# The chunk inverse of a delta-rule recurrence: levels over half the columns, one half of the state kept in PSUM

## The reference

```python
def step(S, inp):
    r_t, w_t, k_t, v_t, kk_t, b_t = inp
    Sa = jnp.einsum('bhij,bhj->bhi', S, -kk_t)
    S = S * w_t[:, :, None, :] + Sa[..., None] * b_t[:, :, None, :] + v_t[..., None] * k_t[:, :, None, :]
    return S, jnp.einsum('bhij,bhj->bhi', S, r_t)

S_final, y = lax.scan(step, wkv0.astype(f32), seq_in)
```

## Time and profile before

| | |
|---|---|
| median of three executions | 1726.22 us |
| the profiled execution, its own time | 1722.33 us |
| its span | 1720.5 us |
| PE busy | 1581.8 us, 92% |
| DVE busy | 1009.6 us, 59% |
| ACT busy | 843.4 us, 49% |
| POOL busy | 578.6 us, 34% |
| mean granted PE clock | 0.974 of 2.4 GHz |

### The profile page before, as it was taken

The page is one execution under the profiler, slowest core; times in us unless marked ns, Lnnn a source line. Parts: engine busy times, 40 slices in busy tenths (PEclk is TensorE's granted clock), DMA queues, the critical chain, the costliest instruction groups (busy, mean ns, idle before and its releaser), DMA issues. The chain is left out here.

```text
span 1720.5 us, 41466 instructions
## 1 busy us (share of the span) xinstructions
PE 1581.8 (92%) x17389; PEld 1499.4 (87%) x17389; DVE 1009.6 (59%) x1718; ACT 843.4 (49%) x1480; POOL 578.6 (34%) x393
## 2 busy tenths in 40 slices
PE   4999999989799899999789999999897989899996
PEld 4999999987588789999789999989776878899995
DVE  3534368695798665443354434968677877544433
ACT  2545455756444555444344444656663446554431
POOL 0433412102266433444233433020215553344440
PEclk9999999999899999999989999999998999999998
DMA  5555557452144445555355555644603463456540
GB/s 174 161 173 177 177 151 220 129 173 79 48 121 124 138 155 176 169 195 178 112 158 173 178 176 183 194 134 145 184 1 101 128 182 101 148 172 196 178 166 26
DMA packets 280490, 256.28 MB, mean 149 GB/s; under 512 B 48022, under 2 KB 268540, under 8 KB 280290
## 3 DMA queue, kind: packets, MB, share of 16 engines
q1 hardware_dynamic: 276538, 252.05, 47.0%
q10 hardware_dynamic: 3768, 1.59, 0.4%
HBM read 242.22 MB, written 11.38 MB: 147 GB/s over the span
## 5 line engine op out<-in xcount | busy, mean ns | idle before, releaser
L223 PE MATMUL ps<-front_h_hi,front_hi 128*128 128x264 f32 x1520 | 447.4, 294 | 35.1 <-DVE front_lo L210 31.2
L224 PE MATMUL ps<-front_h_lo,front_hi 128*128 128x264 f32 x1520 | 436.9, 287 | 0.0
L225 PE MATMUL ps<-front_h_hi,front_lo 128*128 128x264 f32 x1520 | 436.5, 287 | 0.0
L210 POOL TENSOR_TENSOR front_lo<-front_raw,front_hi 128x1024 fp32r<-128x1024 f32 (+2 forms) x90 | 217.5, 2416 | 574.2 <-ACT front_hi L203 574.2
L203 ACT ACTIVATE front_hi<-front_raw 128x1024 fp32r<-128x1024 f32 (+2 forms) x238 | 246.7, 1039 | 274.7 <-PE ps L225 237.0
L223 PEld LDWEIGHTS ps<-front_h_hi,front_hi 128*128 128x128 f32 x1520 | 291.6, 192 | 44.8 <-issue 41.2
L210 POOL TENSOR_TENSOR out_lo<-out_raw,out_hi 128x1024 fp32r<-128x1024 f32 (+1 forms) x84 | 198.8, 2369 | 310.8 <-ACT out_hi L203 310.8
L224 PEld LDWEIGHTS ps<-front_h_lo,front_hi 128*128 128x128 f32 x1520 | 291.9, 192 | 0.8
L225 PEld LDWEIGHTS ps<-front_h_hi,front_lo 128*128 128x128 f32 x1520 | 290.2, 191 | 0.1
L203 ACT ACTIVATE out_hi<-out_raw 128x1024 fp32r<-128x1024 f32 (+1 forms) x168 | 173.2, 1038 | 220.9 <-PE ps L225 178.0
L210 DVE TENSOR_TENSOR front_lo<-front_raw,front_hi 128x1024 fp32r<-128x1024 f32 (+1 forms) x148 | 180.0, 1217 | 118.7 <-ACT front_hi L203 118.7
(11 more groups left out here) (375 smaller groups left out, 3346.9 us busy)
## 6 DMA issues: line engine op xcount, KB each, us to landing
front_raw<-in_w_in SPq DMA_DIRECT2D x50, 1024.0 KB, 5.3
front_raw<-in_ffn_w_in SPq DMA_DIRECT2D x44, 1024.0 KB, 5.7
out_raw<-in_ffn_w_in SPq DMA_DIRECT2D x44, 1024.0 KB, 5.6
back_sample_rows<-row_scratch SPq DMA_DIRECT2D x160, 128.0 KB, 3.0
out_raw<-in_w_out SPq DMA_DIRECT2D x16, 1024.0 KB, 6.3
front_raw<-in_ffn_w_out SPq DMA_DIRECT2D x16, 896.0 KB, 4.6
out_raw<-in_ffn_w_out SPq DMA_DIRECT2D x16, 896.0 KB, 4.6
front_raw<-in_ffn_w_out SPq DMA_DIRECT2D x8, 1024.0 KB, 5.0
```

The costliest lines, as they stand in the source:

```text
L210: eng.tensor_tensor(self.lo[n % self.RING][:, 0:k, 0:w], self._raw(n), self.hi[n % self.RING][:, 0:k, 0:w].bitcast(F32), ALU.subtract).the ...
L223: pe.matmul(out, hi[:, j, 0:w], x_hi[:, j], start=start and j == 0, stop=False)
L224: pe.matmul(out, hi[:, j, 0:w], x_lo[:, j], start=False, stop=False)
L225: mm = pe.matmul(out, lo[:, j, 0:w], x_hi[:, j], start=False, stop=stop and j == k - 1)
```

## The change

Five things change, all in `back_stage`, for both layers.

- Level `i` only fills the columns of the early half of every block pair in `x` and of the late half in `xt`. `part_of(a, i, late)` picks these 32 of every 64 columns, in runs of `b` columns. `level_t1` and both products of `level_u` now stream 32 columns in place of 64; their number stays.
- `t1` gets one buffer per level (`t1_pair`, `t1_rest`), set to zero once by POOL; `t1_copy` writes only the early half.
- `turn_x` writes bank UB and leaves its accumulation open. The U product adds to it there (`add=True`), so `x` is summed up in PSUM.
- DVE's addition to `x` goes. In its place `x_update(l, i)` on ACT copies the changed half of bank UB to `x`; it stands directly ahead of `t1_copy(l, i + 1)`. `level_t1(l, i + 1)` waits for it by `x_in`.
- DVE's addition to `xt` covers half the columns.

```diff
+    def part_of(a, i, late):
+        b = LEVELS[i]
+        return a.rearrange("p (n two t) -> p n two t", two=2, t=b)[:, :, late]
+
+    columns = lambda a: a.rearrange("p q t -> p (q t)")
...
-        t1 = st.sb("n_x", [P, 4, C])
+        t1_pair = st.sb("n_x_first", [P, 2, 4, C])
+        t1_rest = at("n_x_rest", 71296, [P, LV - 2, 4, C])
+        t1 = lambda i: t1_pair[:, i] if i < 2 else t1_rest[:, i - 2]
...
+                pool.memset(t1_pair[:], 0.0).then_inc(s("t1_zero"), 1)
                 for g in range(RT + 1):
                     l = g - 1
+                    if g == 1:
+                        pool.wait_ge(s("tok_ps"), 2)
+                        pool.memset(t1_rest[:], 0.0).then_inc(s("t1_zero"), 1)
...
-                    act.activation(t1[:].rearrange("p q t -> p (q t)"), ps[:, T1B, 0:4 * C], ACT.Copy).then_inc(s("t1_in"), 1)
+                    if p == 0:
+                        act.wait_ge(s("t1_zero"), 1 if i < 2 else 2)
+                    act.activation(part_of(columns(t1(i)), i, 0), part_of(ps[:, T1B, 0:4 * C], i, 0), ACT.Copy).then_inc(s("t1_in"), 1)
...
+                def x_update(p, i):
+                    act.wait_ge(s("u_ps"), (LV - 1) * p + i + 1)
+                    act.activation(part_of(columns(x[:, p % 2]), i, 0), part_of(ps[:, UB, 0:4 * C], i, 0), ACT.Copy).then_inc(s("x_in"), 1)
...
                     if 0 <= l < RT:
+                        x_update(l, 0)
                         t1_copy(l, 1)
...
                     if 0 <= l < RT:
+                        x_update(l, 3)
                         t1_copy(l, 4)
                         rv_copy(l)
...
                 def update(p, i):
-                    four = lambda b: ps[:, b, 0:4 * C].rearrange("p (q t) -> p q t", q=4)
-                    if i < LV - 1:
-                        ...
-                        dve.tensor_tensor(x[:, p % 2], x[:, p % 2], four(UB), ALU.add).then_inc(s("x_up"), 1)
                     dve.wait_ge(s("ut_ps"), LV * p + i + 1)
                     if i:
                         dve.wait_ge(s("xt_up"), LV * p + i)
-                    dve.tensor_tensor(xt[:, p % 3], xt[:, p % 3], four(UB + 1), ALU.add).then_inc(s("xt_up"), 1)
+                    changed = part_of(columns(xt[:, p % 3]), i, 1)
+                    dve.tensor_tensor(changed, changed, part_of(ps[:, UB + 1, 0:4 * C], i, 1), ALU.add).then_inc(s("xt_up"), 1)
...
-                def blocks(at, left, right):
+                def blocks(at, left, right, i, late, add=False):
+
                     for q in range(4):
                         for w in half:
-                            mm = pe.matmul(ps[w, at, q * C:(q + 1) * C], left[w, q], right[w, q], start=True, stop=True)
+                            mm = pe.matmul(part_of(ps[w, at, q * C:(q + 1) * C], i, late), left[w, q], part_of(right[w, q], i, late),
+                                           start=not add, stop=True, skip_group_check=add)
...
                     if p:
-                        pe.wait_ge(s("t1_in"), LV * p)
+                        pe.wait_ge(s("x_in"), LV * p)
...
                     pe.wait_ge(s("lev_done"), n + 1)
-                    if i:
-                        pe.wait_ge(s("x_up"), (LV - 1) * p + i)
+                    pe.wait_ge(s("x_in"), n + 1)
+                    if n:
                         pe.wait_ge(s("t1_in"), n)
-                    else:
-                        pe.wait_ge(s("x_in"), p + 1)
-                    blocks(T1B, lev[:, n % 2], x[:, p % 2]).then_inc(s("t1_ps"), 1)
+                    blocks(T1B, lev[:, n % 2], x[:, p % 2], i, 0).then_inc(s("t1_ps"), 1)
```

More of the change, by code:

```diff
@@ L1674, in t1_copy @@
                         act.wait_ge(s("ut_ps"), n)
-                    act.activation(t1[:].rearrange("p q t -> p (q t)"), ps[:, T1B, 0:4 * C], ACT.Copy).then_inc(s("t1_in"), 1)
+                    if p == 0:
+                        act.wait_ge(s("t1_zero"), 1 if i < 2 else 2)
+                    act.activation(part_of(columns(t1(i)), i, 0), part_of(ps[:, T1B, 0:4 * C], i, 0), ACT.Copy).then_inc(s("t1_in"), 1)
                 def x_copy(p):
                     act.wait_ge(s("x_ps"), p + 1)
-                    act.activation(x[:, p % 2].rearrange("p q t -> p (q t)"), ps[:, T1B, 0:4 * C], ACT.Copy).then_inc(s("x_in"), 1)
+                    act.activation(columns(x[:, p % 2]), ps[:, UB, 0:4 * C], ACT.Copy).then_inc(s("x_in"), 1)
+                def x_update(p, i):
+                    act.wait_ge(s("u_ps"), (LV - 1) * p + i + 1)
+                    act.activation(part_of(columns(x[:, p % 2]), i, 0), part_of(ps[:, UB, 0:4 * C], i, 0), ACT.Copy).then_inc(s("x_in"), 1)
                 def rv_copy(p):
@@ L1789, in _ @@
                     if 0 <= l < RT:
+                        x_update(l, 1)
                         t1_copy(l, 2)
@@ L1800, in _ @@
                     if 0 <= l < RT:
+                        x_update(l, 2)
                         t1_copy(l, 3)
@@ L1875, in update @@
                 def update(p, i):
-                    four = lambda b: ps[:, b, 0:4 * C].rearrange("p (q t) -> p q t", q=4)
-                    if i < LV - 1:
-                        dve.wait_ge(s("u_ps"), (LV - 1) * p + i + 1)
-                        if i:
-                            dve.wait_ge(s("x_up"), (LV - 1) * p + i)
-                        else:
-                            dve.wait_ge(s("x_in"), p + 1)
-                        dve.tensor_tensor(x[:, p % 2], x[:, p % 2], four(UB), ALU.add).then_inc(s("x_up"), 1)
                     dve.wait_ge(s("ut_ps"), LV * p + i + 1)
@@ L2063, in turn_x @@
                     pe.wait_ge(s("start"), p + 1)
+                    pe.wait_ge(s("turned"), 2)
                     if p:
-                        pe.wait_ge(s("t1_in"), LV * p)
+                        pe.wait_ge(s("x_in"), LV * p)
                     for q in range(4):
                         for w in half:
-                            mm = pe.matmul(ps[w, T1B, q * C:(q + 1) * C], xt[w, p % 3, q], eye2[w], start=True, stop=True)
+                            mm = pe.matmul(ps[w, UB, q * C:(q + 1) * C], xt[w, p % 3, q], eye2[w], start=q == 0, stop=False,
+                                           skip_group_check=True)
                     mm.then_inc(s("x_ps"), 1)
@@ L2086, in level_u @@
                     if i < LV - 1:
-                        blocks(UB, xt[:, p % 3], t1[:]).then_inc(s("u_ps"), 1)
-                    blocks(UB + 1, t1[:], xt[:, p % 3]).then_inc(s("ut_ps"), 1)
+                        blocks(UB, xt[:, p % 3], t1(i), i, 0, add=True).then_inc(s("u_ps"), 1)
+                    blocks(UB + 1, t1(i), xt[:, p % 3], i, 1).then_inc(s("ut_ps"), 1)
                 def gv(p):
@@ L2236, in _ @@
                         solve(c)
-                    if g == 1:
-                        pe.wait_ge(s("turned"), 2)
                     if 0 <= l < RT:
```

## The result

| | before | after |
|---|---|---|
| median of the runs, us | 1725.43 (4 runs) | 1795.36 (4 runs, 1793.70 to 1816.01) |
| ratio to before, 95% interval | | 1.0434 (1.0400 to 1.0468) |
| profiled execution, own time / span, us | 1722.33 / 1720.5 | 1794.48 / 1792.6 |
| mean granted clock of TensorE | 0.974 | 0.937 |

Slower, as forecast, but by 70 us where I had forecast 40, and 7 us above the range. (The medians alone give 1.0405; one of the four runs took 1816.01 us.) Every reason that I had given for a wait was there. What I had priced far too low is the clock, and I had left out turns in which it falls.

What follows compares the result with a forecast made beforehand. PE's own program was taken to bound a steady turn, DVE the turn g = 1. Per layer 16.9 + 2.5 + 1.4 - 0.6 = +20.2 us, two layers +40.4 on 1722.33: 1763 us, range 1736 to 1788.

Steps and rivals of the forecast that it cites:

- Half columns save PE nothing: Level products on PE: 32 columns take as long as 64, 0 us saved per product, bounds 0 and 0.23.
- The rival in which columns count as time: Level products: each 0.23 us shorter, -51.5 us against +40.4 of waits, so 1711 us; chance 0.11.
- The waits of a steady turn: Turns g = 3 to 7: level_t1 waits for copies in ACT's queue, +3.37 us per turn.
- The sum of the waits: All turns of both recurrences: +20.2 us per layer, +40.4 us for two layers.
- Waits alone: Both recurrences: only PE's waits for ACT's copies cost time, own range 1750 to 1776 us; chance 0.60.
- Part 1 of the forecast: Level products on PE with half the columns: 0 us saved per product, at most 3.2 us per turn.
- The clock: Ten steady turns: PE's clock falls too, one stretch of 1.45 us each, +14.5, 1777 us; chance 0.22.
- The argument against the clock: Turn g = 1 runs at full clock with PE busy 78%, and the new turn would have 80%.
- DVE: DVE's additions to xt get 0.13 us shorter; DVE sheds some 2.3 us per turn and idles more.
- All hidden: ACT reaches the copies earlier than placed, so the waits are hidden: 1722 to 1728 us; chance 0.05.

Runs made afterwards that it cites:

- e6_late_stream: The changed kernel with the level products streaming all 64 columns again, copies and their places on ACT as in the change: 1756.39 us, ratio 1.0191.
- e1_early: The changed kernel with the four x_update copies moved ahead in ACT's program, nothing else: 1727.60 us, ratio 1.0020.
- the thin fillers: The changed kernel with extra matmuls of 8 columns, in blocks of eight, put into PE's waits ahead of level_t1: 1819.15 us, ratio 1.0551.
- e10_half_copies: The kernel before with T1's copy and DVE's two additions at half columns, products at 64, x still added up by DVE: 1720.53 us, ratio 0.9981.
- e5_early_stream: The changed kernel with the four x_update copies moved ahead on ACT and level products of 64 columns: 1717.32 us, ratio 0.9958.

## Why the prediction was wrong in size, step by step

- **Half columns save PE nothing.** Right. Forecast 0 us per product, measured 0.02. The rival in which columns count as time (1711) is out.
- **The waits of a steady turn.** Right nearly to the term, read at full clock. `level_t1(l, 1)` starts 4.03 us after the turn's first product (533.14 to 537.17); before it was 2.61 (531.10, where the window of the earlier trace rows begins, to 533.71), and the forecast put 1.45 on it, 4.06. `level_u(l, 1)` to `level_t1(l, 2)` 2.61, forecast 2.61. `level_t1(l, 2)` to `level_u(l, 2)` 1.02, forecast 1.07. On to `level_t1(l, 3)` 2.72, forecast 2.73. From `level_u(l, 3)` to `level_t1(l, 4)` 2.01, forecast 1.97. The copy takes 0.27, forecast 0.28. Turn 18.27, forecast 18.4. The releaser was to be ACT's copy; the trace names others, and only ACT's own rows show it. PE started 0.09 to 0.11 us after that copy's end, where I had 0.06.
- **The sum of the waits.** `e6_late_stream` has the waits at PE's old clock. It is 32 us slower than the kernel before by the medians; its profiled span is 37.6 longer (1758.1 against 1720.5). The forecast was +40.4. Turn by turn in the first recurrence, g = 1 came to -0.4 (forecast -0.6), g = 2 to +1.7 (+1.4), g = 8 to +2.4 (+2.5), and the five steady turns together to +14.3 (+16.9): I had put the figures of g = 5 on all five, but g = 3, 4 and 7 lost only 2.4, 3.0 and 2.1.
- **"Waits alone" as the likeliest case, at 0.60.** This failed. It holds only for products of 64 columns. With the edit that Part 1 of the forecast had priced at nothing, the same waits came with 39 us more.
- **The clock.** This is the step that failed: the rival was there, with the sign right, but its term was too small and covered too few turns. I priced it with one half-clock stretch of 1.45 us in each steady turn, +14.5 in all, and nothing in the other turns. The stretch came from the turn with the weight loads. Measured: the changed kernel is 39 us above `e6_late_stream` by the medians, and its profiled recurrences are 36 us longer (26.6 and 9.4). Of these, 22.8 are in the ten steady turns, most of them in the three turns at 0.60 of the first recurrence (25.9 us in place of 18.5 in two of them). The turn g = 1 has 10.1, in both layers together, and g = 8 has 3.2.
- **The argument against the clock.** It made 0.22 too low: g = 1 runs at full clock with PE busy 78%. That row had products of 64 columns. `e6_late_stream` confirms it for them: 80% busy, clock 1.00, in g = 1 of the first recurrence and in the steady turns g = 3 to 6 (g = 1 of the second has 0.91). With 32 columns g = 1 itself ran at 0.63, and steady turns with PE 80% busy stood next to turns at 0.60. The row answered the wrong question. I had even written that no row shows what counts as activity in products of half the columns, and should have let that lack widen the range: the upper end ought to have had whole half-clock turns in it. The rows before would have priced one: 4.56 / 3.11 = 1.47, times 14.7, less 14.7, is some 7 us, and 7.6 was measured. They could not have told how many such turns there would be.
- **DVE.** Right: DVE is busy for 9.61 us of a turn of 18.27. Its additions fell from 0.42 us to 0.29, the 0.13 that I had taken; these are the five of the turn at full clock:

```profile
L1902 DVE TENSOR_TENSOR back_inverse_t<-back_inverse_t,ps 128x128 f32<-128x128 f32 x5 | 1.4, 287 | 6.6 <-PE ps L2075 6.6
```

- **All hidden.** Out: only by moving the copies does it come near (`e1_early`, 1727.6).

The Trainium skill ("TensorE: Matmul & The Clock Gate", section "What's actually happening") has the slow clock as the default that activity lifts, and says that the gate goes by how busy PE has been. The rows agree with the first: with the same waits the clock of the first recurrence is 0.99 with 64 columns and 0.75 with 32. They do not bear out the second, if busy is what the profile calls busy: the thin fillers had PE busy 95% of the time, at 0.79.

## What to carry to other kernels

When an edit thins the matmuls of a stage without shortening them, price the clock as well as the time: compare a full-clock stretch with a half-clock one of the same kernel, do so for every turn in which the engine has idle time (the first one included), and do not take a row with the old shapes as proof for the new ones. A copy that is moved to an idle engine can cost what stands ahead of it in that engine's order; find its earliest position before judging the move, since four moved instructions were worth 39 to 68 us here. And test such a change in its parts: here the half-size copies gain (`e10_half_copies`), the late order and the short products lose. Whether the PSUM sum with early copies gains anything on top is not shown: `e5_early_stream` and `e10_half_copies` are 3 us apart, and their intervals overlap.

## What was not expected of the hardware

- The starts of the 16 records of a product cover 0.44 us with 32 columns and 0.46 us with 64. The granted clock of the first recurrence was 0.75 with the former and 0.99 with the latter, at the same waits.
- The lower clock came in some turns and not in others of the same program: 25.85, 18.27, 25.89 and 18.26 us in a row, with mean clocks of 0.60 and 1.00 in the first recurrence, and none of the steady turns at 0.60 in the second.
- PE busy 95% of the time, in part with matmuls of 8 columns, had a clock of 0.79; busy 80% with 64-column products, 0.99.
- A copy from PSUM of 128 elements per partition in short runs takes 0.27 us on ACT, no more than a contiguous one of the same size.
